# First feed-forward of a decoder layer on one Trainium2 core: two pairs of up units multiplied chunk by chunk, with the eight first conditioning units between them

## The reference, cut to what matters

```python
ada = (silu(c) @ w_ada + b_ada).reshape(n, 3, 3, 1024)      # 9 conditioning rows, 72 column blocks of 128
mod(t, i)  = t * (1 + ada[:, i, 1]) + ada[:, i, 0]
post(t, y, i) = layernorm(ALPHA * t + ada[:, i, 2] * y, ln_g[i], ln_b[i])
x = post(x, 0.5 * (silu(mod(x,0) @ f1g) * (mod(x,0) @ f1u)) @ f1d, 0)     # first feed-forward
x = post(x, mixer(mod(x, 1)), 1)                                          # attention and convolution
x = post(x, 0.5 * (silu(mod(x,2) @ f2g) * (mod(x,2) @ f2u)) @ f2d, 2)     # second feed-forward
```

## Time and profile before

| | |
|---|---|
| median of 3 runs | 867.71 us (867.45 to 868.11) |
| the profiled execution's own time | 866.49 us |
| its span (first to last instruction) | 864.4 us |
| mean granted TensorE clock | 0.992 of 2.4 GHz |
| TensorE busy | 826.8 us, 96% |
| DVE, ACT, POOL busy | 465.7, 341.6, 254.6 us |
| moved by DMA | 197.44 MB, 228 GB/s over the span |

### The profile page before, as it was taken

One profiled execution on the slowest core, in us unless ns is written; L12 is line 12 of the kernel. 1 busy time (PEld: TensorE's weight loads), 2 busy tenths in 40 slices (PEclk: granted clock), 3 DMA queues, 4 the chain that ended last, 5 costly groups with the idle time before them and its releaser, 6 DMA issues.

```text
span 864.4 us, 16835 instructions
## 1 busy us (share of the span) xinstructions
PE 826.8 (96%) x6708; PEld 736.5 (85%) x6708; DVE 465.7 (54%) x711; ACT 341.6 (40%) x473; POOL 254.6 (29%) x309
## 2 busy tenths in 40 slices
PE   5999999999999999999988989989999999999997
PEld 3799999998899899887665656559799999999996
DVE  0654434434335678536797797449844444444454
ACT  2432333333123585455344333355753333332240
POOL 2030000000002308999999999101100000000030
PEclk9999999999999999999999999999999999999998
DMA  9996786784945435347998999999444444645421
GB/s 300 348 364 229 266 289 223 270 290 158 329 136 178 160 123 195 99 146 236 379 355 286 356 364 361 349 357 377 134 145 148 146 146 146 177 135 161 144 74 61
DMA packets 159601, 197.44 MB, mean 228 GB/s; under 512 B 11907, under 2 KB 132985, under 8 KB 159525
## 3 DMA queue, kind: packets, MB, share of 16 engines
q1 hardware_dynamic: 150445, 187.94, 65.7%
q10 hardware_dynamic: 8800, 8.43, 3.0%
q0 software_dynamic: 288, 0.14, 0.1%
HBM read 193.67 MB, written 3.17 MB: 228 GB/s over the span
## 4 chain that ended last, share of the span: by engine, by line
PE 81%; DVE 8%; DMA 5%; ACT 2%; issue 2%; POOL 1%; SPq 0%; DVEq 0%; ACTq 0%; POOLq 0%
PE bank L1744 19%; PE bank L1746 19%; PE bank L1745 19%; PE bank L2033 5%; PE bank L2058 3%; PE bank L1705 2%; PE bank L2142 2%; DVE kT L1470 2%; DMA araw<-in_w_ada 1%; DMA xrow<-in_x_sample 1%; DMA raw<-in_ffn_wg 1%; DMA araw<-in_cache_v 1%; PE bank L1776 1%; DVE yT L1397 1%; DVE wlo L1156 1%
## 5 line engine op out<-in xcount | busy, mean ns | idle before, releaser
L1156 DVE TENSOR_TENSOR wlo<-raw,whi 128x2048 fp32r<-128x2048 f32 (+1 forms) x80 | 184.1, 2302 | 222.4 <-ACT whi L768 222.2
L1744 PE MATMUL bank<-mh,whi 128*128 128x320 f32 x816 | 254.5, 312 | 0.0
L1746 PE MATMUL bank<-mh,wlo 128*128 128x320 f32 x816 | 252.2, 309 | 0.0
L1745 PE MATMUL bank<-ml,whi 128*128 128x320 f32 x816 | 252.2, 309 | 0.0
L768 ACT CAST whi<-raw 128x2048 fp32r<-128x2048 f32 (+1 forms) x80 | 148.6, 1858 | 202.4 <-PE bank L1746 196.1
L1744 PEld LDWEIGHTS bank<-mh,whi 128*128 128x128 f32 x816 | 153.3, 188 | 5.9 <-issue 5.8
L1745 PEld LDWEIGHTS bank<-ml,whi 128*128 128x128 f32 x816 | 153.3, 188 | 0.1
L1746 PEld LDWEIGHTS bank<-mh,wlo 128*128 128x128 f32 x816 | 153.3, 188 | 0.0
L1744 PE MATMUL bank<-hh,whi 128*128 128x320 f32 x352 | 109.6, 311 | 0.0
L1745 PE MATMUL bank<-hl,whi 128*128 128x320 f32 x352 | 108.8, 309 | 0.0
L1746 PE MATMUL bank<-hh,wlo 128*128 128x320 f32 x352 | 108.8, 309 | 0.0
(11 more groups left out here) (308 smaller groups left out, 1072.2 us busy)
## 6 DMA issues: line engine op xcount, KB each, us to landing
araw<-in_w_ada SPq DMA_DIRECT2D x24, 1024.0 KB, 6.6
raw<-in_ffn_wg SPq DMA_DIRECT2D x22, 1024.0 KB, 9.1
raw<-in_ffn_wu SPq DMA_DIRECT2D x22, 1024.0 KB, 10.4
raw<-in_ffn_wd SPq DMA_DIRECT2D x16, 1024.0 KB, 5.4
raw<-in_cache_k SPq DMA_DIRECT2D x56, 256.0 KB, 4.5
raw<-in_cache_v SPq DMA_DIRECT2D x42, 256.0 KB, 7.1
raw<-in_w_in SPq DMA_DIRECT2D x10, 1024.0 KB, 5.3
raw<-in_w_ada SPq DMA_DIRECT2D x8, 1024.0 KB, 11.2
```

The costliest lines, as they stand in the source:

```text
L1156: dve.tensor_tensor(wl(slot_w(phase, u))[:, 0:size], landed(phase, u)[:, 0:size], wh(slot_w(phase, u))[:, 0:size].bitcast(F32), ALU.subtra ...
L1744: pe.matmul(bank[:, b, 0:T], wh(slot)[:, c], h_, start=(start and n == 0), stop=False)
L1745: pe.matmul(bank[:, b, 0:T], wh(slot)[:, c], l_, start=False, stop=False)
L1746: ins = pe.matmul(bank[:, b, 0:T], wl(slot)[:, c], h_, start=False, stop=(stop and n == len(parts) - 1))
```

## The change

Units 0 to 3 get a place of their own (`whi3`, `wlo3`, and the second to third slots) and are loaded, rounded and subtracted in quarters of two chunks (`load_piece`, `hi_piece`, `lo_piece`), 256 KB each. TensorE multiplies the quarters as stages: `early_stage(pair, s)` has the 6 matmuls of each unit and chunk for all four column blocks of pair 0 (24 matmuls), for pair 1 for three of its four (18), since bank 7 holds the conditioning; the fourth block follows at the end (`early_rest`). The eight conditioning units have a landing of their own with three slots (`aland`). Their product writes the four column groups of 64 columns each (32 matmuls of 64 columns in place of 8 of 256), and a DVE transpose (`early_turn`) takes the place of ACT's copy and TensorE's turn. A product waits for the transposition of the one before (`early_flip`), a load for the product that frees its slot (`ada_used`). No slab is hosted by pairs 0 and 1 any more; down units 1, 2, 4, 6, 8, 10 host slabs 26 to 31. The fold is split in two (`fold(0)` at 20 conditioning units, `fold(1)` in the first norm, behind three memsets of POOL). Tokens are loaded and turned first.

```diff
+EARLY = 4
+ADA_UP = 2
+ADA_LAND = 3
+STAGES = NCH // 2
+PIECES = [(0, 0), (1, 0), (0, 1), (1, 1), (2, 0), (3, 0), (2, 1), (3, 1), (0, 2), (1, 2), (2, 2), (3, 2)]
-ADA_HOSTS = {1: 30, 2: 31}
+ADA_HOSTS = {1: 26, 2: 27, 4: 28, 6: 29, 8: 30, 10: 31}
...
 SP
-            for u in range(ADA0):
...
+            def load_early_ada(u):
+
+                if u >= ADA_LAND:
+                    sp.wait_ge(ada_used, u - ADA_LAND + 1)
+                sp.dma_start(aland[:, u % ADA_LAND, :].rearrange("p (k c) -> p k c", c=UC),
+                             cols(i["w_ada"], slice(UC * ADA_ORDER[u], UC * ADA_ORDER[u] + UC))).then_inc(aland_in[u % ADA_LAND], 16)
...
+            load_early_ada(0)
+            load_early_ada(1)
+            for u, s in PIECES[0:2]:
+                load_piece(u, s)
+            load_early_ada(2)
+            load_early_ada(3)
+            for u, s in PIECES[2:8]:
+                load_piece(u, s)
+            load_early_ada(4)
+            load_early_ada(5)
+            load_early_ada(6)
+            load_early_ada(7)
+            for u, s in PIECES[8:12]:
+                load_piece(u, s)
+            for u in range(EARLY):
+                load_piece(u, STAGES - 1)
...
 ACT
+            for u, s in PIECES[0:2]:
+                hi_piece(u, s)
+            split_m(0)
+            for u, s in PIECES[2:6]:
+                hi_piece(u, s)
+            split_m(1)
+            for u, s in PIECES[6:8]:
+                hi_piece(u, s)
+            split_m(2)
+            split_m(3)
+            for u, s in PIECES[8:12]:
+                hi_piece(u, s)
+            for u in range(EARLY):
+                hi_piece(u, STAGES - 1)
...
 DVE
+            def early_turn(u):
+
+                dve.wait_ge(ada_used, u + 1)
+                q = 2 * QG * (u % 4)
+                turned = rows[:, u // 4, q:q + 2 * QG]
+                dve.transpose(turned, bank[:, 7, 2 * QG * u:2 * QG * u + 2 * QG]).then_inc(early_flip, 1)
+                dve.wait_ge(early_flip, u + 1)
...
+            early_chunks(0)
+            for u, s in PIECES[0:2]:
+                lo_piece(u, s)
+            early_lows(0)
+            for u, s in PIECES[2:4]:
+                lo_piece(u, s)
+            early_chunks(1)
+            early_lows(1)
+            for u, s in PIECES[4:8]:
+                lo_piece(u, s)
+            early_chunks(2)
+            early_lows(2)
+            early_chunks(3)
+            early_lows(3)
+            for u, s in PIECES[8:12]:
+                lo_piece(u, s)
+            for u in range(EARLY):
+                lo_piece(u, STAGES - 1)
...
 PE
+            def early_stage(pair, s):
+
+                pe.wait_ge(piece_lo, PIECES.index((2 * pair + 1, s)) + 1)
+                for kk in (2 * s, 2 * s + 1):
+                    for target in early_targets(pair):
+                        early_product(target, kk)
...
+            turn_x()
+            turn_params()
+            ada_product(0)
+            keep_clock_early(8)
+            ada_product(1)
+            keep_clock_early(8)
+            early_stage(0, 0)
+            ada_product(2)
+            ada_product(3)
+            keep_clock_early(4)
+            early_stage(0, 1)
+            early_stage(1, 0)
+            ada_product(4)
+            early_stage(1, 1)
+            ada_product(5)
+            ada_product(6)
+            ada_product(7)
+            early_stage(0, 2)
+            early_stage(1, 2)
+            early_last(0)
+            early_last(1)
+            early_rest()
```

More of the change, by code:

```diff
@@ L228, in slot_w @@
         return 1 + u
+    if phase[0] == UP1[0] and u < EARLY:
+        return u
     return u % SLOTS
@@ L241, in slot_before @@
         return (WOUT[0] + 1, WOUT[0] + 2, WOUT[0] + 3, UP2[0])[u]
+    if phase[0] == UP1[0] and u < 6:
+        return u - EARLY
     return phase[0] + u - SLOTS
@@ L424, in build @@
         N_EARLY = 2 + DB + 1
-        X_AT = 1
-        def mod_chunks(u):
-            return range(u - 2, u) if u and u % 2 == 0 else ()
         block = es.enter_context(nc.Block())
@@ L442, in up_pairs, with first_bank @@
             body(10, 10, 0)
+        def first_bank(ffn, pair_):
+            return 4 if ffn == 0 and pair_ == 1 else 0
         def part_of(a_, g=0):
@@ L524, in load_first_up @@
             def load_first_up(pair, pair_, g):
-                for x in range(2):
-                    load_ada(ADA0 + 2 * pair + x, ADA0 + 2 * pair_ + x, g)
+                if pair_ >= ADA_UP:
+                    for x in range(2):
+                        load_ada(ADA0 + 2 * (pair - ADA_UP) + x, ADA0 + 2 * (pair_ - ADA_UP) + x, g)
                 if pair_ < 9:
@@ L718, in _ @@
             pool.memset(qo[:, :, :, :], 0.0).then_inc(q_zero, 1)
+            fold(1)
             pool.wait_ge(st_in, 2)
@@ L825, in body @@
                             act.wait_ge(hr, 2 * pair + cc - 1)
[L826 to L829 removed]
+                        act.activation(tmp[:, cc, :], bank[:, first_bank(ffn, pair_) + cc, 0:T], ACT.Silu).then_inc(sr, 1)
+                    if ffn == 0 and pair_ < 2:
+                        if pair_ == 0:
+                            hi_next(4)
+                            hi_next(5)
+                    else:
+                        if pair_:
+                            hi_next(2)
+                        hi_next(3)
                     for cc in range(2):
@@ L1735, in _, with early_targets, early_product @@
-            ada_turn(ADA0 - 1, ADA0 - 1)
-            keep_clock_early(6)
+                    pe.matmul(bank[:, 6, 0:P], ident, ident, start=True, stop=True)
+            def early_targets(pair):
+                return [(4 * pair + 2 * x + cc, 2 * pair + x, cc, ((g_ready, u_ready)[x][0], w_used)[cc])
+                        for x in range(2) for cc in range(2) if (pair, x, cc) != (1, 1, 1)]
+            def early_product(target, kk):
+                b, slot, cc, done = target
+                c = slice(UC * kk + P * cc, UC * kk + P * cc + P)
+                pe.wait_ge(mh_ready, kk + 1)
+                pe.wait_ge(ml_ready, kk + 1)
+                pe.matmul(bank[:, b, 0:T], wh(slot)[:, c], mh[:, kk, :], start=kk == 0, stop=False)
+                pe.matmul(bank[:, b, 0:T], wh(slot)[:, c], ml[:, kk, :], start=False, stop=False)
+                return pe.matmul(bank[:, b, 0:T], wl(slot)[:, c], mh[:, kk, :], start=False, stop=kk == NCH - 1)
@@ new lines, in early_stage, with early_last @@
+            def early_stage(pair, s):
[3 more added lines that the diff above has]
+                        early_product(target, kk)
+            def early_last(pair):
+                targets = early_targets(pair)
+                for x in range(2):
+                    pe.wait_ge(w_lo, 2 * pair + x + 1)
+                    for kk in (NCH - 2, NCH - 1):
+                        for target in targets[2 * x:2 * x + 2]:
+                            ins = early_product(target, kk)
+                            if kk == NCH - 1:
+                                ins.then_inc(target[3], 1)
@@ new lines, in early_rest @@
+            def early_rest():
+                pe.wait_ge(ada_out, ADA0)
+                for kk in range(NCH):
+                    ins = early_product((7, 3, 1, w_used), kk)
+                ins.then_inc(w_used, 1)
+            pe.wait_ge(c_silu, 1)
+            turn_x()
[7 more added lines that the diff above has]
+            ada_product(3)
@@ L1789, in modulated_products @@
                     rest(NCH - 1, target).then_inc(target[3], 1)
-            def first_unit(slot, done, w0, ml0):
-                pe.wait_ge(w_hi, w0 + 1)
-                for q in range(NCH):
-                    pe.wait_ge(ml_ready, ml0 + q + 1)
-                    for cc in range(2):
-                        c = slice(UC * q + P * cc, UC * q + P * cc + P)
-                        pe.matmul(bank[:, cc, 0:T], wh(slot)[:, c], mh[:, q, :], start=q == 0, stop=False)
-                        pe.matmul(bank[:, cc, 0:T], wh(slot)[:, c], ml[:, q, :], start=False, stop=False)
-                pe.wait_ge(w_lo, w0 + 1)
-                for q in range(NCH):
-                    for cc in range(2):
-                        c = slice(UC * q + P * cc, UC * q + P * cc + P)
-                        ins = pe.matmul(bank[:, cc, 0:T], wl(slot)[:, c], mh[:, q, :], start=False, stop=q == NCH - 1)
-                        if q == NCH - 1:
-                            ins.then_inc(done[cc], 1)
             def m_parts(order):
```

237 lines of the change are left out of this document (110 added, 127 removed).

## The result

The changed kernel takes 870.33 us (median of 19 runs, 866.83 to 874.05), the kernel before 867.45 (19 runs on the same chip, 863.82 to 872.13): ratio 1.0035, interval 1.0021 to 1.0049. It is slower by 2.9 us, where 5.3 us were forecast. Its profiled execution took 872.98 us, so the traces differ by more (6.8 us of span) than the medians do.

A forecast was written before the change was run, and what follows sets the result against it. TensorE, 96% busy, was taken as the bound, with only the head able to give time. Walk and moved slabs +2.2, fallen clock 2.5 and port 0.6 gave +5.3 on 867.7: 873.0 us, range 866.5 to 879.

The forecast's parts named there:

- the string: Before stage (0,2): conditioning, ACT and DVE's quarters run on one line, leaving TensorE 4.4 us of work in 11.
- T: Start of TensorE's stage (0,2), put at 53.5 us; 108 matmuls, 15.9 us, then remain before pair 2.
- The start of the walk: Program start: product 0 to 15.4, eight keepers (filler matmuls) to 17.3, stage (0,0) at 22.7 us.
- The price of a product: Each early conditioning product of 32 matmuls of 64 columns on TensorE: 1.45 us with the drain.
- I take nothing: Clock falls in the gaps before stages (0,0) and (0,1): up to 1.7 us each, counted as zero.
- rival 2: Clock falls also before stages (0,0) and (0,1), or products take 1.64: 876.4, up to 879 us; chance 0.19.
- The clock behind T: TensorE's clock has fallen when stage (0,2) starts, after the pause; loss taken as 2.5 us.
- Landings: DMA loads: load 7 lands at 44.9, third quarters by 47.9, before ACT needs them; 4 us idle DMA costs nothing.
- if the walk were quicker, they would be next: Head: the DMA landings would be the next bound if the chain of products and stages ran quicker.
- POOL against DVE: Shared port, POOL's `scale_x` beside DVE's subtraction of unit 5: 0 or 1.3 us, taken as 0.6.
- The head: Program up to pair 2: +5.3 us in all, counting 3.72 for the four slabs moved behind it.
- The price of moving the slabs to down units is nothing: Down stage: four slabs moved there cost nothing extra, as their loads have at least one 7 us unit of cover.

The follow-up runs named there:

- e3: Changed kernel plus sixteen keepers (matmuls without use) between the last conditioning product's transposition and stage (0,2); ratio 1.0030 to the kernel before.
- e1: Changed kernel with the third quarters rounded and subtracted ahead of chunks 6 and 7 of the modulation; ratio 1.0018 to the kernel before.
- e5: e4 with product 4 ahead of stage (1,0) and products 5 and 6 ahead of stage (1,1); ratio 0.9999 to the kernel before.
- e7: e5 with the six down-stage slabs hosted in three pairs (down units 2, 5, 8); 864.32 us, ratio 0.9968 to the kernel before.
- e8: e7 with units 4 and 5 landing in conditioning places 0 and 3, once products 4 and 7 free them; ratio 0.9966 to the kernel before.
- e10: e8 with its twenty small keepers (matmuls without use) replaced by ten of 512 columns; 860.67 us, ratio 0.9938 to the kernel before.
- e4: Changed kernel with both the third quarters first (e1) and a fourth conditioning landing place (e2); ratio 0.9979 to the kernel before.
- e2: Changed kernel with a fourth landing place for conditioning units, so load 7 waits for product 3, not 4; ratio 1.0040 to the kernel before.
- e11: e8 without any keepers (matmuls without use); 860.01 us, ratio 0.9933 to the kernel before.
- a2: The changed kernel unaltered, timed again later in six runs; ratio 1.0056 to the kernel before.
- e9: e8 with 15 and 9 keepers (matmuls without use) in place of 8 and 4; 866.75 us, ratio 1.0000 to the kernel before.

## Why the prediction was right

The measured median of 870.33 lies in the range (866.5 to 879), and "slower" had 0.76. The forecast of 873.0 was 2.7 us too high for the median, and its forecast for the profiled execution (871.8) 1.2 too low. The mechanism on which it rested, the string and then the low clock, is the measured one; that the sum came so near is in part errors that cancel. By its own steps:

- **T: right.** Forecast 53.5, measured 54.42, and for the reason given: conditioning, ACT and DVE on one line, and then 4.5 us of nothing (forecast 4.7). Product 7 was put at 47.3 to 48.8, and ran from 48.85.
- **The start of the walk: too short by 0.9.** Product 0 and its keepers were put at 1.5 and 1.9 us and took 1.94 and 2.89, so stage (0,0) began at 23.62 for 22.7. The forecast named 1.94 as the bound before the clock has risen and didn't take it. Eight of the thirteen profiled executions did without it, so this part is chance.
- **The price of a product: size off.** 1.45 was taken; from product 1 on it is 1.10 with its drain, 1.03 at the pitch, just under the lower bound of 1.07. The 21 ns per record of the earlier trace rows become 16, so the 25 ns of the Trainium skill (TensorE: Matmul & The Clock Gate, section "Wait — 56ns, not 53.3ns?") disagree more than I saw. Six of them behind product 1 made the walk some 2 us too long on paper.
- **"I take nothing" for falls of the clock before stages (0,0) and (0,1): wrong.** That was rival 2's condition. It fell from 24 to 28 (0.57), though there were keepers: stage (0,0) took 5.23 us, where e3, whose clock held, took 3.69. That is 1.5, near the 1.7 priced there; before stage (0,1) nothing fell. With the slow start the walk was 2.7 us late at product 2 (28.85 for 26.2), and the short products brought that back to 1.6 at product 7 and 0.9 at T, which is why T looks better than its terms.
- **The clock behind T: right.** Forecast 2.5; pair 2 begins at 72.24, which is 17.8 behind T in place of 15.9: 1.9, the same as by e3.
- **Landings: wrong by a hair.** "Load 7 lands at 44.9, the third quarters land by 47.9, all before ACT comes to them": it landed at 48.6, 7.0 us behind its issue and not 5, since the quarters issued behind it shared the engines with it, and the last third quarter at 51.5 (by e1). ACT came at 52.4, so nothing was lost by it yet; but "4 us of idle DMA cost nothing in themselves" hid that a second bound lay 1 us below the first, and e1 ran into it. Where I named it ("if the walk were quicker, they would be next") it was right, without a number.
- **POOL against DVE: mechanism right, size 0 for 0.6.** DVE's subtraction kept its 2.28 at 69.78, POOL's `scale_x` was drawn to 8.64 us (69.97), and `hl` came through in 6.50 for two. TensorE did not wait.
- **The head:** +5.0 for the forecast's +5.3, both with 3.72 for the moved slabs; with the 4.1 that two pairs cost it is +5.4.
- **"The price of moving the slabs to down units is nothing": the step that failed.** It is 1.2 us against the kernel before (217.5 - 212.6 - 3.72): 0.7 for hosting alone what had stood in pairs, 0.4 because two rows of 1.86 are not all that two pairs cost, 0.1 for a landing. The cover of 7 us was asked about loads only; what an interruption of TensorE's row of 0.147 us matmuls costs, once for each host, was not. And the cover was no proof for the loads: the second slab hosted there waited 0.9 us for its landing, in the kernel before as well (0.8).

That the medians differ by 2.9 us and these parts add up to 6.2 has a part that stays open. The profiled execution of the changed kernel is one of its slower ones (872.98, 2.7 above its median), that of before one of its quicker ones. In the start of the walk executions do differ, as the table has it, and both profiles of the changed kernel have the slow start, up to 2 us. How often which happens wasn't measured, as only one execution of each is profiled.

One thing the forecast had no term for: the supply of instructions. In the changed kernel it cost 0.44 us at most, hidden in a wait, so it is no part of this result; it is a reason why the reordered versions (e5, e7, e8) gave less than their T on paper, with stops of 2.0 to 2.3 us, and fewer instructions gave the last step, from 0.9966 (e8) to 0.9938 (e10), whose intervals just overlap. The largest step was e4's, from 1.0035 to 0.9979.

## What to carry to other kernels

When a walk hands over between engines many times, put next to the binding line the time at which the second line (here the landings behind one freed place) would bind, since an edit that undoes the first gains only their distance: one edit brought T forward by 0.9 us, the other left the pause before it as it was, and together they brought it forward by 4.3. Compare such marks from a station in front of the edit, as the start of a program alone can differ by 2 us from one execution to the next. An interruption of a dense row of matmuls has a price per interruption, so host small work in pairs, and look whether a second row in place of a second host also takes a wait away. Count TensorE's instructions in dense small work: a filler or a product of 64 columns costs supply as well as time, and a stop marked "issue" that stays at the same count of instructions while the code around it moves is not scheduling.

## What the runs showed of the hardware that was not expected

- TensorE stops for 0.3 to 2.7 us with nothing to wait for at fixed places of its stream: behind 317, 439 and 561 to 564 matmul records from product 0 on, at the last of them in nine kernels (changed, e2, e5 to e11), which went on between 45.7 and 48.1. Each of the twelve stops ends 1.3 to 1.6 us behind the end of a 16 KB packet of an instruction queue; where the packet had ended 2.0 us or more before TensorE came there (a2, e3, e4), there was no stop. What makes a packet late stays open; that it is the full DMA engines (about 350 GB/s) was not tried.
- Matmul records of 64 columns in a 32-column group start every 16 ns (64 records in 1.03 us) at a clock of 1.00.
- Keepers don't decide alone whether the clock falls. In the ten kernels with 8 keepers before stage (0,0), TensorE idle for 1.9 us behind them, it fell at stage (0,0) or shortly before in nine and held in one (e3). With the gap filled all but 0.3 and 0.2 us (e9, e10) it held, in one execution of each. Under the sixteen keepers of e3 it fell too (0.57 from 48 to 52), behind a stretch with 1.79 busy us of 4.
- A slab of 16 small matmul records costs 1.21 us in a dense row when it stands alone and 1.03 in a pair.
- Behind an empty queue 1 MB took 7.0 us from issue to landing, with more loads issued right behind it: the queue had moved some 1.95 MB by then.
